# Tighter pacing of the first token tile's second-layer chores, and half of its output projection placed between the last expert sums

## The reference, cut to what matters

```python
def chunk(args):                       # PEER: 128 experts for each token
    xc, ec, gc = args
    u = expert_u[ec]
    act = jax.nn.gelu(jnp.einsum('cd,ced->ce', xc, u).astype(jnp.float32))
    return jnp.einsum('ce,ced->cd', gc * act, expert_v[ec])
...
x = x + gt2 * peer_ffn(...)            # then the final norm of block one
x = rmsnorm(x, ln_final_g)
...
def hybrid_layer(x, ...):              # block two, on all 256 tokens
    h = rmsnorm_2(x, pre_norm_w)
    proj = jnp.einsum('bsd,de->bse', h, w_in)
    ...                                # attention, gated delta rule, gates
    merged = jax.nn.sigmoid(gate_a) * y_a + jax.nn.sigmoid(gate_b) * y_b
    out = jnp.einsum('bsd,de->bse', merged, w_out)
    return x + rmsnorm_2(out, post_norm_w)
```

## Time and profile before

| what | value |
| --- | --- |
| median of three runs | 1291.72 us (1291.27 to 1292.57) |
| the profiled execution | 1300.05 us, of which the profile's span is 1298.2 us |
| mean granted clock of TensorE | 0.93 of full speed |
| TensorE busy | 1094.3 us (84%) |
| VectorE, ScalarE, GpSimd busy | 793.2, 448.3, 294.0 us |
| indirect fetches | 256, 268.45 MB |

### The profile page before, as it was taken

The page is one execution under the profiler, slowest core; times in us unless marked ns, Lnnn a source line. Parts: engine busy times, 40 slices in busy tenths (PEclk is TensorE's granted clock), DMA queues, the critical chain, the costliest instruction groups (busy, mean ns, idle before and its releaser), DMA issues.

```text
span 1298.2 us, 14207 instructions
## 1 busy us (share of the span) xinstructions
PE 1094.3 (84%) x5194; PEld 549.9 (42%) x5194; DVE 793.2 (61%) x1853; ACT 448.3 (35%) x1249; POOL 294.0 (23%) x261
## 2 busy tenths in 40 slices
PE   6989996787887676759897779968999799998998
PEld 2968674333243222213332334423443345555543
DVE  5465756988864999654357667666664367645201
ACT  1113203655442444444253344434334223322201
POOL 0000002434334443433323333333322000000000
PEclk9988967999988889989989989998999799999999
DMA  9995705998999999999999999999999475433573
GB/s 389 326 407 197 275 1 212 366 395 353 421 369 422 421 422 405 405 422 376 422 419 422 421 421 411 421 421 386 391 420 423 196 275 212 178 130 142 217 299 136
DMA packets 63665, 433.16 MB, mean 334 GB/s; under 512 B 6979, under 2 KB 10348, under 8 KB 11884
## 3 DMA queue, kind: packets, MB, share of 16 engines
q0 software_dynamic: 36864, 268.45, 50.7%
q1 hardware_dynamic: 26336, 162.81, 32.2%
q10 hardware_dynamic: 396, 0.99, 0.2%
HBM read 431.17 MB, written 1.06 MB: 333 GB/s over the span
## 4 chain that ended last, share of the span: by engine, by line
PE 55%; DMA 18%; DVE 17%; ACT 6%; issue 2%; POOL 1%; another core or an unknown queue 0%; SPq 0%; POOLq 0%; DVEq 0%; ACTq 0%
PE ps L1117 20%; DMA AR<-in_puv,idx 16%; PE ps L1072 11%; DVE AR L1689 6%; PE ps L766 6%; PE ps L1231 3%; PE ps L988 2%; PE ps L1016 2%; DMA W<-in_w_in 1%; PE ps L801 1%; PE ps L1098 1%; POOL AR L2474 1%; PE ps L935 1%; ACT av L2223 1%; DMA W<-in_w_mod 1%
## 5 line engine op out<-in xcount | busy, mean ns | idle before, releaser
L2474 POOL DMA_INDIRECT AR<-in_puv,idx x256 | 293.7, 1147 | 699.5 <-PE ps L1072 437.2
L1072 PE MATMUL ps<-AR,acc 128*64 128x512 f32 x912 | 288.8, 673 | 115.1 <-ACT acc L2106 112.9
L1689 DVE CUSTOM_DVE_ANT_0 AR<-AR,mixT 128x1024 f32<-128x1024 f32 x128 | 153.1, 1222 | 68.1 <-DMA AR<-in_puv,idx 67.9
L1072 PEld LDWEIGHTS ps<-AR,acc 128*64 128x64 f32 x912 | 72.6, 147 | 284.0 <-ACT acc L2106 187.7
L1117 PE MATMUL ps<-W,AR 128*128 128x512 f32 x416 | 188.7, 596 | 0.7 <-ACT AR L2106 0.7
L1689 DVE CUSTOM_DVE_ANT_0 AR<-AR,tok 128x1024 f32<-128x1024 f32 x128 | 152.8, 1221 | 49.4 <-DMA AR<-in_puv,idx 49.2
L1117 PE MATMUL ps<-W,hT 128*128 128x512 f32 x320 | 160.3, 632 | 2.8 <-DVE PT L1996 2.8
L2221 ACT ACTIVATE av<-av 128x1 f32<-128x1 f32 x256 | 51.4, 201 | 310.6 <-DVE av L1689 306.6
L1117 PEld LDWEIGHTS ps<-W,AR 128*128 128x128 f32 x416 | 75.5, 190 | 77.4 <-issue 75.3
L1117 PEld LDWEIGHTS ps<-W,hT 128*128 128x128 f32 x320 | 58.5, 199 | 77.7 <-issue 72.9
L2106 ACT ACTIVATE acc<-fold,av 128x64 f32<-128x64 f32 x228 | 79.4, 348 | 7.4
(11 more groups left out here) (449 smaller groups left out, 1317.1 us busy)
## 6 DMA issues: line engine op xcount, KB each, us to landing
W<-in_w_in SPq DMA_DIRECT2D x90, 1024.0 KB, 15.5
W<-in_w_mod SPq DMA_DIRECT2D x24, 1024.0 KB, 14.1
W<-in_wba SPq DMA_DIRECT2D x8, 1024.0 KB
W<-in_wbb SPq DMA_DIRECT2D x8, 1024.0 KB
W<-in_wo SPq DMA_DIRECT2D x8, 1024.0 KB
W<-in_w_out SPq DMA_DIRECT2D x4, 1024.0 KB, 5.9
W<-in_wq SPq DMA_DIRECT2D x4, 1024.0 KB
AR<-in_puv,idx POOLq DMA_INDIRECT x256
```

The costliest lines, as they stand in the source:

```text
L1072: t = mm(of(("E", a, c))[64 * g:64 * g + 64, :], dg_at((2 * p + g) % NDG, late), GB[:, places[g], D + c * 512:D + c * 512 + 512], start=(m ...
L1689: ttr(GB[:, n, 0:D], GB[:, n, 0:D], H2[a][g], 1.0, 0.0, MUL, ADD, av[:, a, c:c + 1]).then_inc(*ve.sig("dot", p, g))
L2474: eng.indirect_dma_start(GB[:, n, :], None, puv, bass.IndirectOffsetOnAxis(ap=idx[:, a, c:c + 1], axis=0)).then_inc(*gp.dma(f"g{n}", "gat" ...
```

## The change

Three edits. The estimate of `rest` is divided by 58 in place of 60, so each step of the second half is given 5.55 us of chores by that estimate in place of 5.36. `merge` begins two steps sooner, at step 122, and as it has eight chores, steps 126 and 127 take the first four of `held`, the four pieces of `o` 0. After the last sum the order is: all of the residual, the roots and `x2_norm`; the four pieces of `o` 1; `norm_h` and `x2_out`; and only then both `o_square` and `finish`. Last, ScalarE computes one unused square root ahead of tile 1's first square, so that the table of that function is loaded there.

```diff
-    share, spent, lag = sum(map(cost, rest)) / 60, 0.0, None
+    share, spent, lag = sum(map(cost, rest)) / 58, 0.0, None
...
-            for _ in range(2 if p >= P - 4 else 0):
-                do(*merge.pop(0))
+            for _ in range(2 if p >= P - 6 else 0):
+                do(*(merge or held).pop(0))
     assert not rest and not merge
     last = second_last()
     do("accumulate", *lag)
-    for front, n in ((6, 5), (2, 5), (2, 1)):
-        for chore in last[:front] + held[:n]:
-            do(*chore)
-        del last[:front], held[:n]
-    assert not held
-    for chore in last:
+    norm, last = last[:10], last[10:]
+    products = [chore for chore in held if chore[0] == "proj"]
+    ends = [chore for chore in held if chore[0] != "proj"]
+    for chore in norm[:8] + products + norm[8:] + ends + last:
         do(*chore)
...
             def x2_add(a, n):
+                if (a, n) == (1, 0):
+                    act(st[:, 46:47], eps, ACT.Sqrt)
                 x2_square(a, n, 0, X[:, a, n * 512:n * 512 + 512], ("x2_add", a, n))
```

## The result

The changed kernel takes 1287.88 us, median of six runs (1286.04 to 1290.79), beside 1292.14 us for the kernel before in the same rounds: a ratio of 0.9966, 95% interval 0.9951 to 0.9982. The forecast was 1287.2 us and 4.5 us less; measured are 0.34% of 1292.14, 4.4 us, with an interval of 2.3 to 6.3 us. The profiled execution took 1286.04 us, with a span of 1284.2 us.

A forecast was written before the change was run, and what follows sets the result against it. The expert loop was taken as bound by the DMA engines, what follows by TensorE. Tail 7.0 us saved, less 0.5 for later sums and 2.0 in the loop, gives 4.5: 1291.72 to 1287.2 us, range 1284.5 to 1290.

The forecast's parts named there:

- Term 1: Between the last sum and tile 1's transposes: eight of 16 output-projection matmuls leave, 14.60 us become 7.6, 7.0 us saved.
- The 0.2 us for the bank: After the last sum: allowance for bank ps7, which comes free only with x2_gate, before o 1 can start.
- The norm's 6.1 us: Tile 1's norm after the last sum: ends 6.1 us after it, 1.5 us ahead of TensorE.
- Term 2: Last sums of the expert loop, with pieces of o 0 between: end 0.5 us later, bounds -0.5 and +1.4.
- The gapless 13.2 us at full clock: From step 125's sum on: three sums and two halves of o 0 without a gap on TensorE, 13.2 us.
- Term 3: Expert loop: fuller steps idle the DMA engines more where buffers are full, so the last fetch lands later, 2.0 us lost.
- a sign of being wrong: Behind tile 1's transposes: the stretch, forecast as long as before, 260 us, would grow.
- Eaten: Loop and last sums: DMA idle time doubles, sums at slow clock; 0.6 us saved, 1291.1 us, no change; chance 0.12.
- slower: Stretch of full buffers: fuller steps hold back two more steps' sums, DMA engines idle 9.9 us more; 1295.1 us; chance 0.09.
- the slab in its extreme form: Loop end: a slab requested at o 0's end lands before the last fetch, delaying it at most 5.0 us; about 1291; chance 0.04.
- well before 1023: End of the loop: the last fetch lands at 1017 to 1021 us; after 1023 the forecast is wrong.
- Good loop: Loop: waits in 880 to 930 no worse, sums at full clock; 7.5 to 9.5 us saved, 1282.2 to 1284.2; chance 0.23.

The follow-up runs named there:

- pace 56: The kernel before with the estimate divided by 56, merge chores from step 120 on, old tail, no pieces in the loop: ratio 1.0008 (0.9990 to 1.0026).

## Why the prediction was right, and which terms were off

The total was right to 0.1 us, and the main mechanism, the shorter tail, as well. That it is so close is luck: the interval of the measurement is 4 us wide, three sizes were off, and they cancel.

**Term 1, the tail.** Forecast 7.0 us, measured 7.3 to 7.7 (14.25 and 14.66 before, 6.97 after). The 0.2 us for the bank were not needed, and eight matmuls at full clock take 7.0 us, not the half of 14.83 that I took, which held a little slow clock. The norm's 6.1 us was 6.06.

**Term 2, the end of the sums.** Forecast 0.5 us later, measured 1.2 to 1.5 us sooner: from the last dot to the last sum's end 4.44 and 4.75 us, 5.94 before. The step that failed is that the slabs are in before the last four fetches. They were in only before the last two. So the sum of step 126 still had to wait 1.72 us, the pieces did not push the last sum, and all that stayed was a side effect: TensorE had no gap ahead of the last sum, which ran in 1.94 us and not in 3.68. That the pieces are what it takes is not shown. The pace alone, without them, has a gap of 1.57 us there and the sum in 1.94 us; pace 56 has 1.77 us and 3.68. The gapless 13.2 us at full clock came true only in the version with both slabs held.

**Term 3, the loop.** Forecast 2.0 us lost, by idle DMA engines in the stretch of full buffers. The profiles at pace 58 have 3 to 7 us more between the first gate and the last dot than three at pace 60 (435.0, 435.4, 434.8; the first profile of before, with 443.4, stands apart). Timed rounds do not tell this cost from nothing (1.0017 and 1.0008, both intervals with 1 in them), so its size rests on these profiles. The reason given was the wrong one: the idling where the buffers are full did not grow (5.1 to 6.3 us at pace 60, 4.5 to 5.6 at pace 58, the first profile of each kernel apart). What the profiles showed in its place is 2.0 us for more of a slab in front of the last fetch, and 2.0 to 2.7 us for an end at which the DMA engines run dry. The slab held back gives 434.1 us at pace 58, with the dry end still there; two steps denser cost nothing more. I had this mechanism as a rival, with the wrong slab: I looked at tile 1's second, which `o` 0 asks for, and took the first to be wholly in front in either case, since it was so in the one profile that I had. By DMA: Bandwidth & Descriptors of the Trainium skill (Queues, rings and completion order) each DMA engine takes turns between queues, and the dots 4.96 us apart with a slab in the queue, 2.48 without, agree. Some idling remains and is not told apart from chance: the changed kernel's first profile lost 4.5 us in 860 to 1000, its second 1.3.

**What I had not in the sum.** In the changed kernel's two profiles the stretch behind the transposes is 262.1 us, 1.65 more than the 260.5 of before; I had taken it as a block. The prediction named this growth as a sign of being wrong, and for this stretch it was. It is TensorE's clock. The timeline of the changed kernel and of the one before at the same place, 31.6 us behind the transposes, and then windows of the changed kernel, with one of the kernel before last:

```profile
1053.68 1.16 PE L1177 MATMUL ps<-K,mixT 128*128 128x1 f32 x8 [1.35 <-DVE mixT L1871]
1054.71 5.26 PE L1115 MATMUL ps<-W,AR 128*128 128x512 f32 x8
```

```profile
1069.36 1.05 PE L1179 MATMUL ps<-K,mixT 128*128 128x1 f32 x8 [1.37 <-DVE mixT L1873]
1070.27 3.68 PE L1117 MATMUL ps<-W,AR 128*128 128x512 f32 x8
```

```profile
1055.00:1056.00 1.00, 1.00 (x2) 0.48 (x2) 0.97 (x2) 0.00 (x0) 0.00 (x0) 0.50 0.00 0
1056.00:1057.00 1.00, 1.00 (x2) 0.38 (x2) 0.41 (x1) 0.00 (x0) 0.00 (x0) 0.50 0.00 0
1057.00:1058.00 1.00, 1.00 (x2) 0.34 (x1) 0.00 (x0) 0.00 (x0) 0.00 (x0) 0.55 0.00 0
...
1071.00:1072.00 1.00, 1.00 (x3) 0.38 (x2) 0.96 (x2) 0.00 (x0) 0.00 (x0) 1.00 0.00 0
```

The same instructions with the same idle time of 1.35 us ahead of them: in one the clock falls to half (0.50), in the other it does not (1.00). Whether the change has a part in it is open: versions with each of its edits are on both sides.

**The ledger.** By profile, the second one of before against the mean of both of after: 7.3 + 1.3 - 5.4 - 1.6 = 1.6 us. By timed medians it is 4.4. The difference is within what single profiles of one kernel scatter, so the sum is not closed to better than some 3 us. The tail's gain is shown by the runs that take the pieces away; the signs of the other terms rest on profiles alone.

**The rivals.** Eaten, slower and the slab in its extreme form fell; the last fetch landed well before 1023 (by 1010.69; 1016.2 with the 5.5 us of the earlier first gate added), and TensorE did not wait ahead of `o` 1. Good loop fell by its time (1282.2 to 1284.2), though both its conditions were nearly met: 880 to 930 lost 4.3 and 1.1 us in the changed kernel's two profiles, and the last two sums ran at full clock. It had no price for slab bytes ahead of the last fetch and for the dry end.

## What to carry to other kernels

In a stretch that is bound by bytes, ask of every transfer whether it must land before the last one that the chain waits for, and issue what need not behind it: holding both slabs (4 MB) back made the changed kernel another 0.4% faster, while asking earlier for what comes later is a part of what its denser pace paid. Then look at what the DMA engines do in the last few us: a hold that leaves them dry won nothing in the kernel before. Dots evenly 2.5 us apart did not show this, the GB/s did. An engine without a long gap also keeps its clock up, which was worth 1.7 us at the last sum here. And before a term is read from where a transfer stands in a profile, look at a second profile of the same kernel.

## What the runs showed of the hardware

At the place 31.6 us behind the transposes the clock fell in both profiles of the changed kernel (after 1.35 us of idling in the first) and in four variants (pace alone, no early root, both slabs held, pieces with both held). It stayed up in both profiles of before (after 1.37 us in the first) and in five variants. With both slabs held it stayed up after 1.94 us ahead of step 125's sum, too. Ahead of the last sum it stayed up after 1.57 us with the pace alone, and was down after 1.77 us at pace 56. Executions of one program differed by 5 us already at the first gate of tile 0 (568.3 and 573.7 in the two profiles of the changed kernel). What sets either was not tried.
